# A Strassen step for 18 of 22 gate and up tile pairs of each FFN layer in a streaming encoder

## The reference, cut to what matters

```python
def rmsnorm(x, g):
    y = x * rsqrt(mean(x * x, axis=-1, keepdims=True) + EPS)
    return y * g

def swiglu(x, w_gate, w_up, w_down):        # 1024 -> 2816 -> 1024
    return (silu(x @ w_gate) * (x @ w_up)) @ w_down

for l in range(2):
    x = x + 0.5 * swiglu(rmsnorm(x, ffn1_norm[l]), ffn1_w_gate[l], ffn1_w_up[l], ffn1_w_down[l])
    x = x + mixer(l, rmsnorm(x, mix_norm[l]))
    x = x + 0.5 * swiglu(rmsnorm(x, ffn2_norm[l]), ffn2_w_gate[l], ffn2_w_up[l], ffn2_w_down[l])
y = rmsnorm(x, final_norm)
```

## Time and profile before

| | |
|---|---|
| three runs | 2167.11, 2163.64, 2164.16 us; median 2164.16 |
| the profiled execution | 2167.01 us; its span 2165.2 us |
| TensorE | 16008 matmuls |
| matmuls in gate, up, conv and attention products (L1106) | 10752 |
| matmuls in Strassen quads (L1255) | 4032 |
| DMA | 226.69 MB, mean 105 GB/s |

### The profile page before, as it was taken

The page is one execution under the profiler, slowest core; times in us unless marked ns, Lnnn a source line. Parts: engine busy times, 40 slices in busy tenths (PEclk is TensorE's granted clock), DMA queues, the critical chain, the costliest instruction groups (busy, mean ns, idle before and its releaser), DMA issues.

```text
span 2165.2 us, 37239 instructions
## 1 busy us (share of the span) xinstructions
PE 2127.7 (98%) x16008; PEld 2083.1 (96%) x16008; DVE 1344.7 (62%) x1781; ACT 835.1 (39%) x1325; POOL 124.3 (6%) x166
## 2 busy tenths in 40 slices
PE   8999999999999999999999999999999999999996
PEld 8999999999999999999999999998888899999996
DVE  6575655865775656558556574675555555757466
ACT  5243433522453433335333342454444433424233
POOL 1000000000000000000000000001000000000001
PEclk9999999999999999999999999999999999999998
DMA  6234352352343343423424334332222142343413
GB/s 196 83 98 128 73 151 69 103 142 86 99 121 95 93 128 92 134 81 107 126 73 114 115 97 142 93 103 84 92 95 92 59 136 75 104 127 92 139 57 93
DMA packets 92916, 226.69 MB, mean 105 GB/s; under 512 B 11024, under 2 KB 25664, under 8 KB 92752
## 3 DMA queue, kind: packets, MB, share of 16 engines
q1 hardware_dynamic: 71712, 186.35, 27.1%
q0 software_dynamic: 17152, 30.26, 7.8%
q10 hardware_dynamic: 3888, 7.70, 1.0%
HBM read 217.17 MB, written 7.09 MB: 104 GB/s over the span
## 4 chain that ended last, share of the span: by engine, by line
PE 86%; DVE 9%; ACT 2%; DMA 2%; issue 1%; DVEq 0%; ACTq 0%; SPq 0%
PE ps L1106 68%; PE ps L1255 13%; DVE w_lo L793 3%; DMA w_quad<-q 1%; PE ps L1187 1%; PE ps L1169 1%; PE ps L1151 1%; ACT w_hi L547 1%; DVE w_quad L800 1%; DVE xg_lo L806 1%; DVE x L953 1%; DMA w_raw<-w 1%; DVE x L947 0%; DVE w_lo L790 0%; DVE x L943 0%
## 5 line engine op out<-in xcount | busy, mean ns | idle before, releaser
L1106 PE MATMUL ps<-xg_hi,w_hi 128*128 128x288 f32 x3584 | 777.8, 299 | 11.4 <-DVE w_lo L790 8.5
L1106 PE MATMUL ps<-xg_hi,w_lo 128*128 128x288 f32 x3584 | 765.3, 295 | 0.0
L1106 PE MATMUL ps<-xg_lo,w_hi 128*128 128x288 f32 x3584 | 765.0, 295 | 0.0
L1106 PEld LDWEIGHTS ps<-xg_hi,w_hi 128*128 128x128 f32 x3584 | 574.4, 189 | 26.2 <-issue 11.4
L1106 PEld LDWEIGHTS ps<-xg_lo,w_hi 128*128 128x128 f32 x3584 | 576.4, 189 | 0.0
L1106 PEld LDWEIGHTS ps<-xg_hi,w_lo 128*128 128x128 f32 x3584 | 576.3, 189 | 0.0
L533 ACT ACTIVATE w_hi<-w_raw 128x1024 fp32r<-128x1024 f32 x232 | 245.5, 1059 | 649.3 <-PE ps L1106 604.1
L915 DVE TENSOR_TENSOR scaled<-ps,rstd 128x576 f32<-128x576 f32 x176 | 133.0, 757 | 454.6 <-PE ps L1106 454.5
L1255 PE MATMUL ps<-hop_hi,w_hi 128*128 128x288 f32 x1344 | 398.2, 296 | 4.0 <-DVE hop_lo L817 1.7
L1255 PE MATMUL ps<-hop_lo,w_hi 128*128 128x288 f32 x1344 | 396.7, 295 | 0.0
L1255 PE MATMUL ps<-hop_hi,w_lo 128*128 128x288 f32 x1344 | 396.0, 295 | 0.0
(11 more groups left out here) (106 smaller groups left out, 1302.1 us busy)
## 6 DMA issues: line engine op xcount, KB each, us to landing
w_raw<-w SPq DMA_DIRECT2D x232, 512.0 KB, 3.5
w_quad<-q SPq DMA_DIRECT2D x180, 256.0 KB, 4.5
w_quad<-q POOLq DMA_DIRECT2D x72, 256.0 KB, 6.3
w_quad<-q SPq DMA_DIRECT2D x80, 192.0 KB, 3.6
w_quad<-q POOLq DMA_DIRECT2D x32, 192.0 KB, 5.1
x<-x_t ACTq DMA_DIRECT2D x8, 288.0 KB, 6.7
k_t<-k_sb ACTq DMA_DIRECT2D x8, 288.0 KB, 2.1
v_t<-v_sb ACTq DMA_DIRECT2D x8, 288.0 KB, 2.5
```

Source lines behind the costliest of these rows:

```text
L1106: mm = pe.matmul(ps[:, 2 * it.slot + b, 0:HALF], wt[:, r, cols], xt[:, k, b * HALF:(b + 1) * HALF], start=(i == 0 and n == 0), stop=(i == ...
```

## The change

In each FFN layer 18 of the 22 pairs of a gate and an up tile are computed by one Strassen step of seven half products too; the four pairs at the start of the layer stay as they were, eight plain tiles, while the layer's norm is found. The chunks are now 6, 8 and 8 deep, and the first chunk holds the four plain pairs and two Strassen ones. A new phase kind "upq" has one quad per pair: its two outputs are the gate tile and the up tile, its depth is the 1024 features in two halves, and its operands are seven combinations of the halves of the gained `x` (`xop_hi`, `xop_lo`), made during the plain tiles (`x_gains`, `x_sums`; one combination is held in free space of `hop` until the plain tiles no longer need its place, and is then copied by `place_t3`). The quad's results leave PSUM as two additions of snapshot and bank; one operation multiplies both by the root; Silu follows in place, in ScalarE's next quad, between snapshots 1 and 2; then comes the product. In the first down quad of a chunk the products go over all but the last depth step first, in the order P1, P5, P2, P4, and then over the last step. All quads of an FFN layer are one run of weight groups. Memory is laid out anew: the raw tiles share `w_quad`, `bt` has five blocks for eight, the squares lie in `bt`, their sum in `rstd`, and the attention's and the convolution's buffers lie in `xop`. The core of the diff:

```diff
-FFN_CHUNKS = (8, 6, 8)
+FFN_CHUNKS = (6, 8, 8)
+PLAIN = 4
...
-T1, B11, B21, B22, T2, T4, T3 = range(PRODUCTS)
+T1, B11, B21, B22, T4, T2, T3 = range(PRODUCTS)
 EARLY, DIRECT, LATE = (0, 2), (2, 4), (4, 7)
+BT_OF = {EARLY: (0, 2), DIRECT: (3, 5), LATE: (0, 3)}
+X_T3, X_SUMS = 1, 4
+X_OF = {B11: 0, T3: X_T3, B21: 2, B22: 3, T1: X_SUMS, T4: X_SUMS + 1, T2: X_SUMS + 2}
+XP = DT // 2
+X_SUMS_AT = {1: 0, 2: 1, 4: 2, 5: 3}
...
-        self.quads = kind in ("down", "conv_out")
+        self.quads = kind in ("upq", "down", "conv_out")
...
-            phases.append(Phase("up", 2 * n, DT, ffn=f, chunk=c, norm=norm if c == 0 else None))
+            whole = PLAIN if c == 0 else 0
+            if whole:
+                phases.append(Phase("up", 2 * whole, DT, ffn=f, chunk=c, norm=norm))
+            phases.append(Phase("upq", n - whole, DT, ffn=f, chunk=c, hid=whole))
...
+                it.p6 = P4 if p.kind != "upq" and it.u == 0 else P6
+                freed += [done + P5, done + it.p6, done + P3]
...
-            parts = ("g1", "g2", "g3", "g4") if it.u else ("g1", "g2", "g4", "g3")
+            parts = ("g1", "g2", "g4", "g3") if it is run[0] else ("g1", "g2", "g3", "g4")
...
-        xg_hi = sb("xg_hi", [P, DT, TOK], F32R)
-        xg_lo = sb("xg_lo", [P, DT, TOK], F32R)
+        at_xop_hi = place
+        xop_hi = sb("xop_hi", [P, PRODUCTS, XP, HALF], F32R)
+        at_xop_lo = place
+        xop_lo = sb("xop_lo", [P, PRODUCTS, XP, HALF], F32R)
...
-        w_raw = sb("w_raw", [P, RAW_SLOTS, DT * P])
-        at_w_quad = place
-        w_quad = sb("w_quad", [P, 7, DT // 2 * P])
+        w_quad = sb("w_quad", [P, 8, DT // 2 * P])
...
-        sumsq = sb("sumsq", [P, TOK])
-        sq = sb("sq", [P, 2, TOK])
-        at_scaled = place
-        scaled = sb("scaled", [P, TOK])
-        scaled2 = sb("scaled2", [P, TOK])
-        at_silu = place
-        silu = sb("silu", [P, TOK])
+        z = sb("z", [P, 2, TOK])
         at_bt = place
-        bt = sb("bt", [P, 8, HALF])
-        at_snap = place
+        bt = sb("bt", [P, 5, HALF])
...
+        sumsq = rstd
+        sq = over("sq", [P, 2, TOK], at_bt)
+        scaled, scaled2 = z[:, 0, :], z[:, 1, :]
...
+            def load_tile(it, last_quad=None):
+                s = it.tile % RAW_SLOTS
+                if last_quad is not None and s == 0:
+                    sp.wait_ge(chain_step, 2 * last_quad.quad + 2)
+                elif last_quad is not None:
+                    sp.wait_ge(w_split, last_quad.steps["g3"].count)
+                elif it.tile >= RAW_SLOTS:
                     sp.wait_ge(w_split, TILES[it.tile - RAW_SLOTS].steps["tile"].count)
-                s = it.tile % RAW_SLOTS
-                sp.dma_start(w_raw[:, s, :], w8[it.tile]).then_inc(raw_loaded[s], 16)
+                sp.dma_start(raw_tile(it), w8[it.tile]).then_inc(raw_loaded[s], 16)
...
+            def x_gains(p, k):
+                pair = XP * p.ffn + k
+                if k == 0 and p.first_done:
+                    act.wait_ge(tile_done, p.first_done)
+                if k == 0 and p.ffn == 3:
+                    for s in range(2):
+                        act.wait_ge(kv_stored[s], 32 + 32 * (DT // 2))
+                act.wait_ge(x_sum_ready, 2 * pair)
+                for part, m in ((snap[:, 0:4:3, :], k), (snap[:, 1:3, :], k + XP)):
+                    act.activation(part, halves(x[:, m, :]), ACT.Copy,
+                                   scale=gain[:, p.norm, m:m + 1]).then_inc(x_gained, 1)
+            def x_sums_hi(p, k):
+                act.wait_ge(x_sum_made, 4 * (XP * p.ffn + k) + 4)
+                act.activation(xop_hi[:, X_SUMS:PRODUCTS, k, :], snap[:, 0:3, :], ACT.Copy).then_inc(x_sum_hi_done, 1)
+                act.activation(hop_hi[:, T3_PAIR, k, :], snap[:, 3, :], ACT.Copy).then_inc(x_sum_hi_done, 1)
+            def place_t3(p):
+                act.wait_ge(tile_done, p.first_done)
+                act.wait_ge(x_sum_ready, 2 * XP * (p.ffn + 1))
+                for xop, hop in ((xop_hi, hop_hi), (xop_lo, hop_lo)):
+                    act.activation(flat(xop[:, X_T3, :, :]), flat(hop[:, T3_PAIR, 0:XP, :]).bitcast(F32),
+                                   ACT.Copy).then_inc(t3_placed, 1)
...
+            def up_quads(p):
+                for it in p.items:
+                    j = p.hid + it.u
+                    if it.first:
+                        place_t3(p)
+                    first_snaps(it, lambda: gate(p, it.u - 1) if it.u else None)
+                    split_hi(it.ahead[0])
+                    if it.u:
+                        pair_parts(p, j - 1)
+                    second_snap(it)
+                    split_hi(it.ahead[1])
+                    split_hi(it.ahead[2])
+                    last_snap(it)
+                    split_hi(it.ahead[3])
+                gate(p, p.n - 1)
+                pair_parts(p, p.hid + p.n - 1)
+            def gate(p, u):
+                act.wait_ge(z_scaled, p.first_silu + u + 1 - PLAIN * (p.ffn + 1))
+                act.activation(scaled, scaled, ACT.Silu).then_inc(silu_done, 1)
...
+            def first_snaps(it, between):
+                bank_b, bank_a = 2 * it.slot + 1, 2 * it.slot + 3
+                if it.quad:
+                    act.wait_ge(tile_read, QUAD_ITEMS[it.quad - 1].evicted + 1)
+                act.wait_ge(tile_done, it.done + P1)
+                act.activation(snap[:, 0, :], ps[:, bank_a, 0:HALF], ACT.Copy).then_inc(snapped, 1)
+                between()
+                if it.quad:
+                    act.wait_ge(tile_read, QUAD_ITEMS[it.quad - 1].evicted + 2)
+                act.wait_ge(tile_done, it.done + P5)
+                act.activation(snap[:, 3, :], ps[:, bank_b, 0:HALF], ACT.Copy).then_inc(snapped, 1)
...
+            def hid_free(p, j):
+                if j % 2 == 0:
+                    dve.wait_ge(pair_ready, 3 * (p.pairs + j // 2))
+            def x_sums(p, k):
+                pair = XP * p.ffn + k
+                dve.wait_ge(x_gained, 2 * pair + 2)
+                dve.tensor_tensor(snap[:, 0, :], snap[:, 0, :], snap[:, 3, :], ALU.subtract).then_inc(x_sum_made, 1)
+                dve.wait_ge(x_sum_made, 4 * pair + 1)
+                dve.tensor_tensor(snap[:, 3, :], snap[:, 2, :], snap[:, 3, :], ALU.subtract).then_inc(x_sum_made, 1)
+                dve.wait_ge(x_sum_made, 4 * pair + 2)
+                dve.scalar_tensor_tensor(snap[:, 2, :], snap[:, 0, :], -1.0, snap[:, 2, :],
+                                         ALU.mult, ALU.subtract).then_inc(x_sum_made, 1)
+                dve.wait_ge(x_sum_made, 4 * pair + 3)
+                dve.scalar_tensor_tensor(snap[:, 1, :], snap[:, 2, :], -1.0, snap[:, 1, :],
+                                         ALU.mult, ALU.subtract).then_inc(x_sum_made, 1)
+            def x_sums_lo(p, k):
+                dve.wait_ge(x_sum_hi_done, 2 * (XP * p.ffn + k) + 2)
+                dve.tensor_tensor(xop_lo[:, X_SUMS:PRODUCTS, k, :], snap[:, 0:3, :],
+                                  xop_hi[:, X_SUMS:PRODUCTS, k, :].bitcast(F32), ALU.subtract).then_inc(x_sum_ready, 1)
+                dve.tensor_tensor(hop_lo[:, T3_PAIR, k, :], snap[:, 3, :],
+                                  hop_hi[:, T3_PAIR, k, :].bitcast(F32), ALU.subtract).then_inc(x_sum_ready, 1)
...
+            def up_quads(p):
+                scales = p.first_silu - PLAIN * (p.ffn + 1)
+                for it in p.items:
+                    g1, g2, g3, g4 = it.ahead
+                    j = p.hid + it.u
+                    shots = 4 * it.quad
+                    split_lo(g1)
+                    if it.u:
+                        pair_parts(p, j - 1)
+                    split_lo(g2)
+                    dve.wait_ge(snapped, shots + 3)
+                    dve.wait_ge(tile_done, it.done + P3)
+                    dve.tensor_tensor(halves(scaled), snap[:, 0:2, :], banks(it.slot), ALU.add).then_inc(tile_read, 1)
+                    split_lo(g3)
+                    dve.wait_ge(snapped, shots + 4)
+                    dve.tensor_tensor(halves(scaled2), snap[:, 2:4, :], banks(it.slot + 1),
+                                      ALU.add).then_inc(tile_read, 1)
+                    dve.wait_ge(tile_read, it.evicted + 2)
+                    dve.tensor_tensor(z[:, :, :], z[:, :, :], rstd[:, :].unsqueeze(1).to_broadcast([P, 2, TOK]),
+                                      ALU.mult).then_inc(z_scaled, 1)
+                    split_lo(g4)
+                    dve.wait_ge(silu_done, p.first_silu + it.u + 1)
+                    dve.wait_ge(z_scaled, scales + it.u + 1)
+                    hid_free(p, j)
+                    dve.tensor_tensor(hidden_place(j), scaled, scaled2, ALU.mult).then_inc(bt_made, 1)
+                    pair_sums(p, j)
+                pair_parts(p, p.hid + p.n - 1)
...
+                    if p.kind == "upq":
+                        hi, lo = xop_hi[:, X_OF[part], k, :], xop_lo[:, X_OF[part], k, :]
+                    else:
```

(28 more changed lines are left out.)

284 lines of the change are left out of this document (168 added, 116 removed).

## The result

The changed kernel takes 2180.1 us (median of four runs, 2178.7 to 2180.8) where the kernel before takes 2164.0 on the same chip: ratio 1.0070, 95% interval 1.0053 to 1.0088. So it is slower by 0.7% (15 us by the ratio, 16 by the medians), though 864 matmuls are gone. The forecast was no change, 2164. Its profiled execution took 2180.78 us, with a span of 2178.8; against the sum of the forecast (2167) 13.8 us are to be explained.

What follows compares the result with a forecast made beforehand. TensorE alone bounds the kernel before; in the new pairs the VectorE and ScalarE feed does. Profiled 2167.0 us, 5 less by chunks, 5 more by clock: 2167; the median is 2.9 lower, so 2164 us, range 2130 to 2192.

Steps and rivals of the forecast that it cites:

- the sum of the forecast (2167): Whole kernel, profiled execution: 2167.0 us before, 5 less by the chunks, 5 more by the clock.
- The feed's cycle of 12.2 us: Gate and up Strassen pairs: VectorE and ScalarE need a mean 12.2 us per pair (12.3 odd, 12.0 even), TensorE 11.2.
- its holes: VectorE in a Strassen pair: empty waits behind weight sums, while ScalarE rounds the new block; 0.62 us left in the second.
- the multiplication: VectorE in each Strassen pair: one 1152-wide operation multiplying gate and up by the root, put at 1.26 us.
- The layer's 352.7 us without the clock: Each FFN layer, from the end of the eighth plain tile: 352.7 us against 354.0 before, gain 1.3 us per layer.
- so I take a third of the places, 5 us: Run ends: TensorE's clock falls behind waits at a third of 8 unhidden places, 1.7 us each, costing 5 us.
- the upper bound that I had worked out from the earlier trace: Ends of runs: the clock falls at all 12, 1.7 us each, 20 us in all.
- the six-deep ends: Four six-deep run ends: VectorE is late there anyway and hides most of the clock's loss, leaving 8 places and 13.6 us.
- the clock falls at every end of a run: Rival, first four products of the down stage behind each run: 1.7 us each, all twelve 2179; slower side 0.38 in all.
- The conv and attention stages keep their instructions: Convolution and attention stages: listed among the parts that cost nothing.
- The x sums, a miss put at about 4 us: Plain tiles: sums of x cost nothing; if their cover failed, a tile would wait about 1 us, 4 us in all.
- Late loads: Rival, weight loads in Strassen runs: each us beyond 15.7 costs 70 us; chance 0.03, in the slower side.

## Why the prediction was wrong, point by point

- *The feed's cycle of 12.2 us*: right in mechanism and size (12.26 and 11.93), with its holes (0.54 and 0.55 us, forecast 0.62) and the multiplication (1.27 from start to start, forecast 1.26). TensorE's waits for snapshot 3 are 1.1 and 0.2 us in turn, where about 1 us in every pair was forecast. The two runs with one more operation show that the loop sets the cycle.
- *The layer's 352.7 us without the clock*: 350.7 in layers 2 to 4, 356.4 in layer 1, in the kernel with the ends filled: 1408.6 for 1410.8 in all. The 354.0 of the kernel before, against which it was set, holds in all four layers by luck: its eight plain tiles take 51.7 us, not 51.2, and the six-deep stage takes 36.1 in layer 1 alone, 35.4 to 35.5 in the others.
- *The clock, "so I take a third of the places, 5 us"*: this step failed. It measured 20.0 us (0.5 of it in layer 1's first pair), the upper bound that I had worked out from the earlier trace rows and set aside. The reason that I gave, that the array is at full load before and behind the gaps, gives no protection; and the six-deep ends hide nothing (layer 2's has 11 matmuls 0.24 us apart, and its stage takes 39.36 us, 37.91 with the end filled). The rival "the clock falls at every end of a run" was what happened, at 11 of 12 ends; that its 2179 lies so near the 2180.1 measured is in part luck, since the other misses below nearly cancel. The rule of the Trainium skill that I had weighed (TensorE: Matmul & The Clock Gate, Part 1: the throttled state is the default, activity lifts it) pointed the same way. 11 of 12 ends agree with it; at the twelfth, behind waits of 2.20 and 0.75 us, the clock stayed.
- *"The conv and attention stages keep their instructions"*: failed, 4.3 us. They do, but not their order: I traced the reordered quad only at the FFN run ends.
- *The x sums, a miss put at about 4 us*: charged nothing. In layer 2 the first split of the Strassen pairs comes 7.7 us behind the last plain tile, as forecast (7.8); in layer 1 it comes at 11.7, and the layer is 5.7 us longer than the others with the ends filled, all of it in these two pairs (30.25 us for 24.20). The wait behind the T3 copies is part of it; whether the x sums make VectorE late there is not shown.

The account against the forecast's sum: 15.0 more for the clock, 2.2 less for the layers without it (layer 1 included), 4.3 for the convolution: 17.1, where 13.8 were measured. The 3.3 too much lie in stages that I held unchanged, above all the convolution's input tiles (1.5 shorter) and the stretch behind the last layer (2.3 shorter). No run looked at those; in the other kernels here, which leave their work as it is, the input tiles take 153.6 to 156.1 us, so the 1.5 is within what these traces differ by. Late loads play no part: with the root's product apart, TensorE runs a stage without a gap at 164 GB/s.

## What to carry to other kernels

Removing work from the engine that sets the pace makes it wait, and each wait can cost more than its length: price the clock at every new wait, near the upper bound for waits as long as the 2.1 to 3.3 us of the table below, until a trace says otherwise. A feeding loop's holes are worth more than its busy share: splitting one operation and moving half of it into a hole, and Silu with it, gave 54 us with all that followed, while the same engine's added work in it was free. When an order is changed in one shared routine, trace every stage that calls it.
